# First gathers of a two-block model's expert layers: an earlier start, other buffers and another order of up and value rows

## The chip, the cores and the metric

The kernel runs on one core of one Trainium2 chip. Its time is device time in microseconds (us) for one launch, and three runs of the kernel before took 1977.8, 1981.58 and 1986.32 us. The engines are TensorE (PE in the profile), VectorE (DVE), ScalarE (ACT), GpSimd (POOL) and SyncE (SP); each runs its own instruction list in order and waits on semaphores for the others.

## The reference

Two transformer blocks run one after the other on 256 tokens of width 1024, in float32. The first block has a token mixer (stick-breaking attention and a gated delta rule), a memory cross attention and an expert layer; the second has a gated linear attention, a spatial gating unit and an expert layer. The expert layer is the same in both:

```
q = (xt @ w_pq).reshape(T, 8, 2, 128)                 # 8 heads, two halves
s = einsum('thpd,hpnd->thpn', q, subkeys)             # 128 scores per half
top_s, top_i = top_k(s, 16)                           # per half
best_s, best_pos = top_k(sums of the 16x16 pairs, 16) # 16 experts per head
act = gelu(einsum('thkd,td->thk', peer_u[expert], xb)) * softmax(best_s)
out = einsum('thk,thkd->td', act, peer_v[expert])
```

Each of the 256 tokens reads 128 rows of `peer_u` ("up rows") and 128 rows of `peer_v` ("value rows"), each 1024 floats, from tables of 16384 rows. For a tile of 128 tokens that is 128 gathers of 128 rows per table, so each block makes 512 gathers of 524,288 bytes.

## The kernel before

The tokens are two tiles of 128 (tile 0 and tile 1). Every dense product streams its weight in units of 256 columns (1 MB) into a ring of four slots, `wring`. ScalarE copies a unit to a rounded high part (`K.high`, `w_hi`), VectorE subtracts to get the low part (`K.low`, `w_lo`), and TensorE multiplies high and low parts. The products of the last dense layer before an expert stage are split: its stage does tile 0, and the expert stage does tile 1 on the side (`SecondTile`: four units of eight chunks of three matmuls, L279; `add`, L290, adds a unit's result to the tokens).

The expert stage is `stage_peer`, run twice (`stage 1` from about 391 us, `stage 2` from about 1283 us in the profile). It opens with a fixed sequence. Tile 0 is normalised (`normalise(0)`), transposed (`columns(0)`: TensorE L2220, then a copy of one half on ScalarE, L2072, and one on VectorE, L1948), multiplied with the first query weight (`query(0)`, L2184) and scored against the keys (`score(0)`, L2197). `first_picks` then finds the first eight experts of head 0 on VectorE and writes their numbers into `ex_idx` (L1933). Gathers are indirect DMAs which GpSimd issues: `gather_u(i)` (L2139) brings up row i, `gather_v(j)` (L2151) value row j; i and j count from 0 to 255, sixteen per head and tile (a group). VectorE forms the dot product of each up row (L1994, signal `u_used`), with one part of the eight-part top-16 search of a later head between two rows. When 16 dot products of a group are there, ScalarE applies gelu (L2099), VectorE forms the weights behind the next group's first row (L1959, `weigh`), ScalarE makes a diagonal matrix of each weight (L2114) and TensorE multiplies it with the value row (L2254, signal `v_used_pe` in the order, `pe_used` in the code).

Buffers set the order of the gathers:

- Up rows 0 to 7 go into slots 0 to 7 of `ex_v` and later ones into `wring`, two rows per ring slot. A ring slot comes free when the query weight in it has been used (`home_free(p)`, a wait on `q_ps`, shown as `heads_out_psum`): rows 8 and 9 need query weight 0 gone, rows 14 and 15 weight 3.
- Value rows have 20 slots: 12 in `ex_v`, used first, and 8 in `value_rows`, which hold query weights 4 to 7 until these have been used. Value row 12 takes the slot of value row 0 again, and so on; `gather_v` waits for TensorE to have used the row before it.
- `ex_v` lies where the layer's `XNT`, `w_hi` and `w_lo` were, so GpSimd waits at its start for all four units of the second tile (`second.done`, shown as `projected`).
- The issue order is written in one loop. Six up rows, then for every further i one `gather_v` and one `gather_u(i)`, but no value row at even i in `LEAD_GROWS`.

```
for i in range(U_AHEAD, ROWS):
    if i not in LEAD_GROWS and i < ROWS - TOPK or i % 2:
        gather_v(j)
        j += 1
    gather_u(i)
```

Query weights 4 to 7 are loaded by SP into `value_rows` while the last dense stage runs, 0 to 3 into `wring` (`load_query`, L172). Before the first expert stage, the stages are the cross attention (`stage_cross_attention`, L1326) and its output product.

Of the kernel before, what the change touches and what calls it, by code (L numbers as in the profile page):

```python
# [47 lines left out]
LEAD_GROWS = range(14, 22)  # L48
# [22 lines left out]
class Core:  # L71
# [1254 lines left out]
def stage_cross_attention(K, qT, kT, v_rows, o_pair, fill):  # L1326
# [10 lines left out]
    with ExitStack() as ctx, nc.Block() as block:  # L1337
# [6 lines left out]
        def _(sp):  # L1344
            K.reload(sp, f[-1] + 2)
# [312 lines left out]
def stage_peer(K, rows, sk, nkeys, sk_dma, table_u, table_v, gelu, after, second, queries, out=None):  # L1658
# [23 lines left out]
    with ExitStack() as ctx, nc.Block() as block:  # L1682
# [63 lines left out]
        def value_slot(n):  # L1746
            return more_rows[:, n, :] if n < VRING - RING else rows[:, n - VRING + RING, :]
# [68 lines left out]
        def _(v):  # L1816
# [206 lines left out]
        def _(act):  # L2023
# [52 lines left out]
            K.high(act, PARTS * (second.units[2][0] + 1))  # L2076
# [49 lines left out]
        def _(pool):  # L2126
            def gather_u(i):
# [4 lines left out]
                sig = u_in[i % RING]  # L2132
                if i < RING:
                    sig = v_in[i]
                elif i < 2 * RING:
                    home_free(pool, (i - RING) // 2)
                else:
                    pool.wait_ge(u_used.sem, u_used.at(i - RING + 1))
                nc.gpsimd.indirect_dma_start(u_row(i), None, table_u, bass.IndirectOffsetOnAxis(  # L2139
                    ap=idx[:, g // PH, i % PER_T:i % PER_T + 1], axis=0)).then_inc(sig.sem, 16)  # L2140

            def gather_v(j):
# [6 lines left out]
                elif n < RING:  # L2149
                    pool.wait_ge(u_used.sem, u_used.at(n + 1))  # L2150
# [16 lines left out]
        def _(pe):  # L2167
# [313 lines left out]
```

## Time and profile before

| | |
|---|---|
| median of three runs | 1981.58 us |
| profiled execution | 1986.98 us |
| its span | 1985.3 us |
| TensorE busy | 1625.2 us (82%) |
| VectorE busy | 1263.5 us (64%) |
| ScalarE busy | 607.6 us (31%) |
| GpSimd busy | 1003.0 us (51%) |
| bytes by software (gather) DMA | 536.94 MB |
| bytes by hardware (SP) DMA | 105.88 MB |

The span is what the engines' records cover, the execution's own time 1.7 us more. Matmuls overlap each other, so TensorE's busy share is no measure of how near it is to its peak. The page's row of GB/s cuts the span in 40 slices of 49.6 us.

### The profile page before, as it was taken

How to read it: one execution, taken by the hardware profiler on the slowest of the kernel's cores; microseconds unless marked ns; L12 is line 12 of the kernel's file. 1: busy time of each engine (PE TensorE's matmuls, PEld its weight loads, DVE VectorE, ACT ScalarE, POOL GpSimd, SP SyncE). 2: the span in 40 equal slices, each digit the busy share in tenths (PEclk: the TensorE clock that was granted, in tenths of full speed). 3: DMA queues.
4: the chain of work that ended last, by engine and by line, in shares of the span. 5: the costliest groups of instructions: out<-in, count | busy, mean ns of one | idle time of the engine just before them, and what ended most of it. 6: DMA issues, size and time to landing. Idle time of an engine off the chain costs nothing. (4 is left out here: it accounts for less than half of the span.)

```text
span 1985.3 us, 22064 instructions
## 1 busy us (share of the span) xinstructions
PE 1625.2 (82%) x7643; PEld 1064.7 (54%) x7643; DVE 1263.5 (64%) x2788; ACT 607.6 (31%) x1151; POOL 1003.0 (51%) x1095
## 2 busy tenths in 40 slices
PE   7999999988898667776577899888898667776687
PEld 7998899874453223332233899874453223332233
DVE  6636375588676666676654536687766666666654
ACT  4464544432122122221221446422122122221121
POOL 3012000056777777777764000057777777777764
PEclk9999899998999888888889999998999888888789
DMA  7531355499999999999999563689999999999997
GB/s 240 177 100 45 127 194 191 159 338 368 410 409 409 409 410 409 409 409 410 409 409 365 182 191 107 212 308 388 409 409 409 409 409 409 409 410 410 410 409 282
DMA packets 243719, 644.22 MB, mean 325 GB/s; under 512 B 19541, under 2 KB 105354, under 8 KB 243610
## 3 DMA queue, kind: packets, MB, share of 16 engines
q0 software_dynamic: 147456, 536.94, 68.2%
q1 hardware_dynamic: 96154, 105.88, 16.7%
q8 instruction: 62, 1.02, 0.2%
q14 instruction: 47, 0.39, 0.1%
HBM read 641.69 MB, written 1.05 MB: 324 GB/s over the span
## 5 line engine op out<-in xcount | busy, mean ns | idle before, releaser
L1994 DVE SCALAR_TENSOR_TENSOR ex_uj<-wring,ps 128x1024 f32<-128x1024 f32 x496 | 605.3, 1221 | 406.0 <-DMA wring<-in_peer_u,ex_idx 402.1
L2254 PE MATMUL ps<-ex_v,ex_diag 128*128 128x512 f32 x1336 | 626.7, 627 | 201.6 <-ACT ex_diag L2114 195.5
L2139 POOL DMA_INDIRECT wring<-in_peer_u,ex_idx x496 | 466.9, 941 | 187.6 <-issue 90.9
L2254 PEld LDWEIGHTS ps<-ex_v,ex_diag 128*128 128x128 f32 x1336 | 266.0, 202 | 549.3 <-issue 324.5
L2254 PE MATMUL ps<-value_rows,ex_diag 128*128 128x512 f32 x664 | 310.6, 623 | 101.1 <-ACT ex_diag L2114 96.0
L2151 POOL DMA_INDIRECT ex_v<-in_peer_v,ex_idx x340 | 320.6, 943 | 114.0 <-issue 88.4
L2254 PEld LDWEIGHTS ps<-value_rows,ex_diag 128*128 128x128 f32 x664 | 131.7, 201 | 273.6 <-issue 165.8
L2139 POOL DMA_INDIRECT ex_v<-in_peer_u,ex_idx x16 | 16.4, 1022 | 474.2 <-PE ps L279 469.9
L204 DVE TENSOR_TENSOR w_lo<-wring,w_hi 128x1024 fp32r<-128x1024 f32 (+1 forms) x160 | 187.5, 1212 | 105.0 <-ACT w_hi L195 104.0
L2114 ACT ACTIVATE ex_diag<-ident,ex_weight 128x128 f32<-128x128 f32 x500 | 159.9, 390 | 191.6 <-PE ps L2254 109.0
L2099 ACT ACTIVATE ex_active<-ex_hidden 128x16 f32<-128x16 f32 x32 | 6.9, 215 | 641.9 <-DVE ex_uj L1994 641.9
L2151 POOL DMA_INDIRECT value_rows<-in_peer_v,ex_idx x172 | 161.3, 938 | 52.5 <-issue 46.1
L195 ACT ACTIVATE w_hi<-wring 128x1024 fp32r<-128x1024 f32 (+1 forms) x160 | 158.1, 1039 | 85.7 <-PE ps L562 37.4
L562 PE MATMUL ps<-XNT_high,w_hi 128*128 128x256 f32 x328 | 94.4, 288 | 2.0 <-DVE XNT_low L671 1.4
L562 PE MATMUL ps<-XNT_low,w_hi 128*128 128x256 f32 x328 | 94.0, 287 | 0.0
L562 PE MATMUL ps<-XNT_high,w_lo 128*128 128x256 f32 x328 | 94.0, 287 | 0.0
L241 PE MATMUL ps<-XNT_high,w_hi 128*128 128x256 f32 x288 | 86.4, 300 | 1.0 <-PEq L502 1.0
L241 PE MATMUL ps<-XNT_low,w_hi 128*128 128x256 f32 x288 | 82.7, 287 | 0.0
L241 PE MATMUL ps<-XNT_high,w_lo 128*128 128x256 f32 x288 | 82.6, 287 | 0.0
L562 PEld LDWEIGHTS ps<-XNT_high,w_hi 128*128 128x128 f32 x328 | 63.6, 194 | 2.8 <-DVE XNT_low L671 1.7
L565 PE MATMUL ps<-w_hi,XNT_high 128*128 128x256 f32 (+1 forms) x208 | 59.7, 287 | 5.5 <-DVE XNT_low L627 3.2
L562 PEld LDWEIGHTS ps<-XNT_low,w_hi 128*128 128x128 f32 x328 | 63.6, 194 | 0.0
(455 smaller groups left out, 2449.2 us busy)
## 6 DMA issues: line engine op xcount, KB each, us to landing
wring<-in_w_in SPq DMA_DIRECT2D x42, 1024.0 KB, 5.6
wring<-in_w_ckv SPq DMA_DIRECT2D x8, 1024.0 KB, 5.2
wring<-in_peer_u,ex_idx POOLq DMA_INDIRECT x496, 15.2
ex_v<-in_peer_v,ex_idx POOLq DMA_INDIRECT x340, 13.9
wring<-in_w_mix_out SPq DMA_DIRECT2D x4, 1024.0 KB, 7.2
wring<-in_w_cq SPq DMA_DIRECT2D x4, 1024.0 KB, 5.2
wring<-in_w_co SPq DMA_DIRECT2D x4, 1024.0 KB, 5.3
value_rows<-in_w_pq SPq DMA_DIRECT2D x4, 1024.0 KB, 10.6
```

The source lines that it names most:

```text
L195: self.nc.scalar.activation(self.part(self.w_hi, m, b), self.raw_part(m, b), ACT.Copy).then_inc(self.named("weights_high").sem, 1)
L204: self.nc.vector.tensor_tensor(self.part(self.w_lo, m, b), self.raw_part(m, b), self.part(self.w_hi, m, b).bitcast(F32), ALU.subtract).the ...
L241: last = mm(ps[:, 6 + u % 2, c * S:(c + 1) * S], w[:, i, c * P:(c + 1) * P], x[:, i, :], start=i == 0 and p == 0, stop=i == KD - 1 and p == 2)
L562: last = nc.tensor.matmul(ps[:, j % BANKS, c * S:(c + 1) * S], w[:, i, off + c * P:off + c * P + P], x[:, i, :], start=start, stop=stop, s ...
L565: last = nc.tensor.matmul(ps[:, j % BANKS, c * m:(c + 1) * m], x[:, i, c * P:(c + 1) * P], w[:, i, :], start=start, stop=stop, skip_group_ ...
L1994: ve.scalar_tensor_tensor(out=uj[i % 2], in0=u_row(i), scalar=1.0, in1=tokens(g // PH), op0=ALU.mult, op1=ALU.mult, accum_out=hidden[:, g ...
L2099: nc.scalar.activation(active[:, g % 2, :], hidden[:, g % 2, :], gelu).then_inc(act_r.sem, 1)
L2114: nc.scalar.activation(diag[:, n % DIAGS, :], K.ident[:, :], ACT.Copy, scale=weight[:, g % 2, s:s + 1]).then_inc(dia.sem, 1)
L2139: nc.gpsimd.indirect_dma_start(u_row(i), None, table_u, bass.IndirectOffsetOnAxis(ap=idx[:, g // PH, i % PER_T:i % PER_T + 1], axis=0)).th ...
L2151: nc.gpsimd.indirect_dma_start(value_slot(n), None, table_v, bass.IndirectOffsetOnAxis(ap=idx[:, j // PER_T, j % PER_T:j % PER_T + 1], axi ...
L2254: last = mm(ps[:, 2 * T + c, :], diag[:, n % DIAGS, :], value_slot(v_slot(j))[:, c * BANK:(c + 1) * BANK], start=j % PER_T == 0, stop=ends)
```

## The change

Four things change, in both expert stages unless said otherwise.

1. The opening of the stage. TensorE transposes the keys first, then does unit 0 of the second tile, tile 0's transposes, unit 1, and `query(0)`; before it did units 0 and 1, keys, transposes, two chunks of unit 2 and `query(0)`. ScalarE and VectorE copy the transposed tokens ahead of their work on unit 2.
2. Buffers of the first up rows. Rows 0 and 1 go into the half of `ex_scores` that belongs to tile 1, which need not wait for any unit; rows 2 to 5 go into `ex_v` slots over unit 2's `w_hi` and `w_lo` and wait for unit 2 alone; rows 6 and 7 go into slots 0 and 1. The wait for all units now stands behind the first six gathers. ScalarE's third score copy waits until rows 0 and 1 have been used. The six slots for up rows come last in the list of free value slots, which still has twelve.
3. Order of gathers. Two more value rows go ahead of up row 8 (three at i = 8), and `LEAD_GROWS` ends at 26 instead of 22, so that up rows 22 and 24 have none ahead of them.
4. In the first block only, query weights 4 and 5 are loaded in the cross attention, into a `value_rows` buffer now split in two halves, and weight 7 with 6 in the product after it. The first `merge` writes into `XNT` instead of a pair of its own, which makes the room.

```diff
-LEAD_GROWS = range(14, 22)
+LEAD_GROWS = range(14, 26)
...
+            for n, p in enumerate((4, 5)):
+                K.reload(sp, f[0] + n)
+                K.load_query(sp, queries[0], p, queries[1])
             K.reload(sp, f[-1] + 2)
...
+        w = 2 * (second.units[2][0] % SPLIT)
+        first_slots = [4 + w, 5 + w, 8 + w, 9 + w, 0, 1]
+        free = [n for n in range(VRING - RING) if n not in first_slots] + first_slots
+        u_slots = {i + 2: n for i, n in enumerate(first_slots)}
         def u_row(i):
-            return value_slot(i) if i < RING else ub[:, (first_row + i) % RING, :]
-        free = [(n + RING) % (VRING - RING) for n in range(VRING - RING)]
+            if i < 2:
+                return scores[:, 1, i * D:(i + 1) * D]
+            return value_slot(u_slots[i]) if i in u_slots else ub[:, (first_row + i) % RING, :]
...
             normalise(0)
+            columns(0)
             K.low(v, PARTS * (second.units[2][0] + 1))
             second.add(v)
             second.add(v)
-            columns(0)
...
+                if k == NT:
+                    act.wait_ge(u_used.sem, u_used.at(2))
...
             first_square(0)
-            K.high(act, PARTS * (second.units[2][0] + 1))
             keys(0)
             columns(0)
...
+                if i == 2:
+                    pool.wait_ge(second.done.sem, second.base + 3)
...
-            pool.wait_ge(second.done.sem, second.base + len(second.units))
             for i in range(U_AHEAD):
                 gather_u(i)
+            pool.wait_ge(second.done.sem, second.base + len(second.units))
             j = 0
             for i in range(U_AHEAD, ROWS):
-                if i not in LEAD_GROWS and i < ROWS - TOPK or i % 2:
+                for _n in range(3 if i == RING else 1 if i not in LEAD_GROWS and i < ROWS - TOPK or i % 2 else 0):
                     gather_v(j)
...
-            second.matmuls(pe, 2 * KD)
             keys(0)
+            second.matmuls(pe, KD)
             columns(0)
-            second.matmuls(pe, 2)
+            second.matmuls(pe, KD)
             query(0)
...
-                pm = K.XNT if queries else split_pair("merged", KD, c)
+                pm = K.XNT
...
-                              queries=(A["w_pq"], value_rows, (4, 5, 6)))
+                              queries=(A["w_pq"], value_rows, (6, 7)))
-            stage_peer(..., second, (A["w_pq"], (1, 7, 2, 3)))
+            stage_peer(..., second, (A["w_pq"], (1, 2, 3)))
```

On ScalarE the opening of stage 1 stands like this before (`XN,ex_ss<-X` is the squares of `normalise(0)`, `sk<-ps` the keys, `ex_xT<-ps` its half of the transposed tokens, `w_hi<-wring` one half of a unit):

```order
227 L2057 ACTIVATE XN,ex_ss<-X 128x1024
228 L2060 ACTIVATE ex_sd<-ex_ss,eps 128x1 [waits mean_square_act]
229 L195 ACTIVATE w_hi<-wring 128x1024 [waits projected,weights_in3]
230 L195 ACTIVATE w_hi<-wring 128x1024
231 L2066 ACTIVATE sk<-ps 128x512 [waits keys_psum]
232 L2072 ACTIVATE ex_xT<-ps 128x4x128 [waits transposed_psum]
233 L195 ACTIVATE w_hi<-wring 128x1024 [waits projected,weights_in0]
234 L195 ACTIVATE w_hi<-wring 128x1024
235 L2030 ACTIVATE ex_query<-ps 128x2x128 [waits heads_out_psum]
```

And on ScalarE at the same place now:

```order
227 L2080 ACTIVATE XN,ex_ss<-X 128x1024
228 L2083 ACTIVATE ex_sd<-ex_ss,eps 128x1 [waits mean_square_act]
229 L2089 ACTIVATE sk<-ps 128x512 [waits keys_psum]
230 L2095 ACTIVATE ex_xT<-ps 128x4x128 [waits transposed_psum]
231 L196 ACTIVATE w_hi<-wring 128x1024 [waits projected,weights_in3]
232 L196 ACTIVATE w_hi<-wring 128x1024
233 L196 ACTIVATE w_hi<-wring 128x1024 [waits projected,weights_in0]
234 L196 ACTIVATE w_hi<-wring 128x1024
235 L2051 ACTIVATE ex_query<-ps 128x2x128 [waits heads_out_psum]
```

The two halves of unit 2 have moved from ahead of the keys and the transposed tokens to behind them.

On GpSimd the first gathers of stage 1 stand like this before (`in_peer_u` is an up row, `in_peer_v` a value row, `x5` five in a row; `experts_picked` is the picks, `heads_out_psum` the use of a query weight):

```order
75 L2139 DMA ex_v<-in_peer_u,ex_idx 128x1024 [waits experts_picked,projected]
76 L2139 DMA ex_v<-in_peer_u,ex_idx 128x1024 x5
77 L2151 DMA ex_v<-in_peer_v,ex_idx 128x1024
78 L2139 DMA ex_v<-in_peer_u,ex_idx 128x1024
79 L2151 DMA ex_v<-in_peer_v,ex_idx 128x1024
80 L2139 DMA ex_v<-in_peer_u,ex_idx 128x1024
81 L2151 DMA ex_v<-in_peer_v,ex_idx 128x1024
82 L2139 DMA wring<-in_peer_u,ex_idx 128x1024 [waits heads_out_psum,experts_picked]
```

And on GpSimd now, up to the same up row 8:

```order
75 L2160 DMA ex_scores<-in_peer_u,ex_idx 128x1024 [waits experts_picked]
76 L2160 DMA ex_scores<-in_peer_u,ex_idx 128x1024
77 L2160 DMA ex_v<-in_peer_u,ex_idx 128x1024 [waits projected]
78 L2160 DMA ex_v<-in_peer_u,ex_idx 128x1024 x3
79 L2172 DMA ex_v<-in_peer_v,ex_idx 128x1024 [waits projected]
80 L2160 DMA ex_v<-in_peer_u,ex_idx 128x1024
81 L2172 DMA ex_v<-in_peer_v,ex_idx 128x1024
82 L2160 DMA ex_v<-in_peer_u,ex_idx 128x1024
83 L2172 DMA ex_v<-in_peer_v,ex_idx 128x1024 x3
84 L2160 DMA wring<-in_peer_u,ex_idx 128x1024 [waits u_used,heads_out_psum,experts_picked]
```

Up row 8 was the twelfth gather and is the fourteenth; the wait for the units has moved behind the first gathers.

Further on in GpSimd's list of stage 1, this is the place before where value row 12 (the first with `v_used_pe`) stands:

```order
95 L2139 DMA wring<-in_peer_u,ex_idx 128x1024 [waits u_used,experts_picked]
96 L2151 DMA ex_v<-in_peer_v,ex_idx 128x1024 [waits u_used]
97 L2139 DMA wring<-in_peer_u,ex_idx 128x1024 [waits u_used] x2
98 L2151 DMA ex_v<-in_peer_v,ex_idx 128x1024 [waits u_used]
99 L2139 DMA wring<-in_peer_u,ex_idx 128x1024 [waits u_used] x2
100 L2151 DMA ex_v<-in_peer_v,ex_idx 128x1024 [waits u_used]
101 L2139 DMA wring<-in_peer_u,ex_idx 128x1024 [waits u_used]
102 L2151 DMA ex_v<-in_peer_v,ex_idx 128x1024 [waits v_used_pe]
103 L2139 DMA wring<-in_peer_u,ex_idx 128x1024 [waits u_used]
```

And GpSimd's list now, from the same up row 16 (`experts_picked`) on:

```order
97 L2160 DMA wring<-in_peer_u,ex_idx 128x1024 [waits u_used,experts_picked]
98 L2172 DMA ex_v<-in_peer_v,ex_idx 128x1024 [waits u_used]
99 L2160 DMA wring<-in_peer_u,ex_idx 128x1024 [waits u_used] x2
100 L2172 DMA ex_v<-in_peer_v,ex_idx 128x1024 [waits v_used_pe]
101 L2160 DMA wring<-in_peer_u,ex_idx 128x1024 [waits u_used] x2
102 L2172 DMA ex_v<-in_peer_v,ex_idx 128x1024 [waits v_used_pe]
```

Value row 12 stood behind up rows 0 to 21 and value rows 0 to 11, 34 gathers; it now stands behind up rows 0 to 18 and the same value rows, 31 gathers.

## Rows read from the trace of the kernel before

**Rows 1.** Page, memory traffic of the core in 40 equal slices of the span.
```profile
GB/s 240 177 100 45 127 194 191 159 338 368 410 409 409 409 410 409 409 409 410 409 409 365 182 191 107 212 308 388 409 409 409 409 409 409 409 410 410 410 409 282
```

**Rows 2.** Windows of stage 1: length, busy time per engine, PE clock, DMA share, GB/s.
```profile
409.45:420.00 10.55, 9.09 (x78) 8.49 (x78) 10.31 (x40) 4.19 (x9) 8.41 (x8) 1.00 0.77 254
420.00:455.00 35.00, 21.54 (x127) 19.42 (x126) 30.74 (x97) 8.34 (x19) 24.85 (x27) 0.83 1.03 409
455.00:475.00 20.00, 20.00 (x51) 10.33 (x50) 17.23 (x50) 2.38 (x9) 12.39 (x14) 0.87 0.89 327
...
485.00:495.00 10.00, 7.93 (x19) 3.29 (x18) 5.00 (x11) 1.50 (x6) 7.49 (x8) 1.00 1.00 366
600.00:700.00 100.00, 73.47 (x159) 31.43 (x158) 62.72 (x154) 18.69 (x47) 75.28 (x82) 0.88 1.03 409
```

**Rows 3.** Timeline, POOL, stage 1: start, duration, instruction [idle before <- releaser].
```profile
409.45 1.17 POOL L2139 DMA_INDIRECT ex_v<-in_peer_u,ex_idx  x1 [239.36 <-PE ps L279]
...
424.33 0.94 POOL L2139 DMA_INDIRECT wring<-in_peer_u,ex_idx  x1 [0.30 <-issue]
...
439.19 0.94 POOL L2139 DMA_INDIRECT wring<-in_peer_u,ex_idx  x1 [1.31 <-PE ps L2184]
...
452.85 0.94 POOL L2139 DMA_INDIRECT wring<-in_peer_u,ex_idx  x1 [0.30 <-issue]
458.28 0.94 POOL L2151 DMA_INDIRECT ex_v<-in_peer_v,ex_idx  x1 [4.49 <-PE ps L2254]
...
480.04 0.94 POOL L2151 DMA_INDIRECT ex_v<-in_peer_v,ex_idx  x1 [1.83 <-PE ps L2254]
```

**Rows 4.** Timeline, POOL, stage 2.
```profile
1301.58 0.93 POOL L2139 DMA_INDIRECT ex_v<-in_peer_u,ex_idx  x1 [230.56 <-PE ps L279]
...
1333.09 0.93 POOL L2139 DMA_INDIRECT wring<-in_peer_u,ex_idx  x1 [3.84 <-PE ps L2184]
...
1346.74 0.94 POOL L2139 DMA_INDIRECT wring<-in_peer_u,ex_idx  x1 [0.30 <-issue]
1349.79 0.94 POOL L2151 DMA_INDIRECT ex_v<-in_peer_v,ex_idx  x1 [2.11 <-PE ps L2254]
```

**Rows 5.** Windows of stage 2.
```profile
1330.00:1345.00 15.00, 4.66 (x30) 4.13 (x28) 11.59 (x34) 2.01 (x4) 9.17 (x10) 0.75 0.93 325
...
1350.00:1360.00 10.00, 10.00 (x23) 4.33 (x22) 8.02 (x22) 0.00 (x0) 7.53 (x8) 0.95 0.94 341
```

**Rows 6.** Timeline, DVE, stage 1: norm, picks, up rows 13 and 16, two weights.
```profile
393.05 1.29 DVE L1942 SCALAR_TENSOR_TENSOR XN<-X,ex_iv,gain 128x1024 f32<-128x1024 f32 x1
...
408.35 0.17 DVE L1933 CAST ex_idx<-ex_sel 128x8 int32<-128x8 f32 x1
...
446.06 1.22 DVE L1994 SCALAR_TENSOR_TENSOR ex_uj<-wring,ps 128x1024 f32<-128x1024 f32 x1 [1.32 <-DMA wring<-in_peer_u,ex_idx]
...
452.17 1.21 DVE L1994 SCALAR_TENSOR_TENSOR ex_uj<-wring,ps 128x1024 f32<-128x1024 f32 x1
453.50 0.23 DVE L1959 SCALAR_TENSOR_TENSOR ex_weight<-ex_active,ex_ginv,ex_gate 128x16 f32<-128x16 f32 x1
...
494.02 0.23 DVE L1959 SCALAR_TENSOR_TENSOR ex_weight<-ex_active,ex_ginv,ex_gate 128x16 f32<-128x16 f32 x1
```

**Rows 7.** Timeline, DVE, stage 2: up row 15.
```profile
1341.67 1.22 DVE L1994 SCALAR_TENSOR_TENSOR ex_uj<-wring,ps 128x1024 f32<-128x1024 f32 x1 [1.51 <-DMA wring<-in_peer_u,ex_idx]
```

**Rows 8.** Timeline, PE, stage 1: first unit, keys, transposes, first query, first value rows.
```profile
391.29 0.36 PE L279 MATMUL ps<-w_hi,XNT_high 128*128 128x256 f32 x1 [0.78 <-PEq L502]
...
397.11 0.60 PE L2210 MATMUL ps<-ident,sk 128*128 128x128 f32 x4
397.55 1.04 PE L2220 MATMUL ps<-ident,XN 128*128 128x128 f32 x8
...
399.46 3.81 PE L2184 MATMUL ps<-ex_xT,wring 128*128 128x128 f32 x32
...
454.22 16.92 PE L2254 MATMUL ps<-ex_v,ex_diag 128*128 128x512 f32 x32 [13.46 <-ACT ex_diag L2114]
```

More of the change, by code:

```diff
@@ L165, in query_home @@
         else:
-            flat = rows[:, 2 * (p - RAW):2 * (p - RAW) + 2, :].rearrange("p r d -> p (r d)")
+            n = 2 * ((p - RAW) % 2)
+            flat = rows[(p - RAW) // 2][:, n:n + 2, :].rearrange("p r d -> p (r d)")
         return flat.rearrange("p (k n) -> p k n", k=KD)
@@ L1323, in stage_delta_rule, with stage_cross_attention @@
     K.end_stage()
-def stage_cross_attention(K, qT, kT, v_rows, o_pair, fill):
+def stage_cross_attention(K, qT, kT, v_rows, o_pair, fill, queries):
     nc = K.nc
@@ L1746, in value_slot, with u_signal @@
         def value_slot(n):
-            return more_rows[:, n, :] if n < VRING - RING else rows[:, n - VRING + RING, :]
-        def u_row(i):
-            return value_slot(i) if i < RING else ub[:, (first_row + i) % RING, :]
-        free = [(n + RING) % (VRING - RING) for n in range(VRING - RING)]
+            if n < VRING - RING:
+                return more_rows[:, n, :]
+            half, row = divmod(n - VRING + RING, RING // 2)
+            return rows[half][:, row, :]
+        w = 2 * (second.units[2][0] % SPLIT)
+        first_slots = [4 + w, 5 + w, 8 + w, 9 + w, 0, 1]
+        free = [n for n in range(VRING - RING) if n not in first_slots] + first_slots
+        u_slots = {i + 2: n for i, n in enumerate(first_slots)}
+        def u_row(i):
+            if i < 2:
+                return scores[:, 1, i * D:(i + 1) * D]
+            return value_slot(u_slots[i]) if i in u_slots else ub[:, (first_row + i) % RING, :]
+        def u_signal(i):
+            if i in u_slots:
+                return v_in[u_slots[i]], 1
+            return u_in[i % RING], len([n for n in range(i % RING, i + 1, RING) if n not in u_slots])
         slots = list(free)
@@ L1765, in u_arrived @@
         def u_arrived(v, i):
-            sig, n = (v_in[i], 1) if i < RING else (u_in[i % RING], i // RING)
+            sig, n = u_signal(i)
             v.wait_ge(sig.sem, sig.at(16 * n))
@@ L1790, in v_arrived @@
             n = v_slot(j)
-            eng.wait_ge(v_in[n].sem, v_in[n].at(16 * (v_use(j) + (2 if n < RING else 1))))
+            eng.wait_ge(v_in[n].sem, v_in[n].at(16 * (v_use(j) + (2 if n in first_slots else 1))))
         @block.sync
@@ L2264, in stage_peer @@
             sig.up(by)
-        for sig in u_in:
-            sig.up(16 * (ROWS // RING - 1))
+        for i in range(ROWS):
+            u_signal(i)[0].up(16)
         for j in range(ROWS):
             v_in[v_slot(j)].up(16)
-        for sig in v_in[:RING]:
-            sig.up(16)
     K.gains_used = first_gain + 1 + after
@@ L2376, in program @@
             sk1 = sb("sk1", [P, 2 * PH, P], ctx=first_keys, side="right")
+            value_rows = [sb("value_rows", [P, RING // 2, D], ctx=rows1, side="right")]
             mem = sb("mem", [P, NT, D], ctx=mem_rows, side="right")
@@ L2400, in program @@
                 fill = Filler(K, K.XNT, u_cq, [qT[:, 2 * h:2 * h + 2, :] for h in range(XH)])
-                stage_cross_attention(K, qT, kT, vr, pair, fill)
+                stage_cross_attention(K, qT, kT, vr, pair, fill, (A["w_pq"], value_rows))
                 mem_rows.close()
-                value_rows = sb("value_rows", [P, RING, D], ctx=rows1, side="right")
+                value_rows.append(sb("value_rows", [P, RING // 2, D], ctx=rows1, side="right"))
                 stage_project(K, rows_jobs(K, u_co[0:RAW], pair, K.X, "add", "V", tiles=1), norm_next=True,
-                              queries=(A["w_pq"], value_rows, (4, 5, 6)))
+                              queries=(A["w_pq"], value_rows, (6, 7)))
             second = second_tile(u_co)
             layer.close()
-            stage_peer(K, value_rows, sk1, 2 * PH, sk_dma, A["peer_u"], A["peer_v"], ACT.Gelu, 2, second, (A["w_pq"], (1, 7, 2, 3)))
+            stage_peer(K, value_rows, sk1, 2 * PH, sk_dma, A["peer_u"], A["peer_v"], ACT.Gelu, 2, second, (A["w_pq"], (1, 2, 3)))
             rows1.close()
@@ L2441, in program @@
                     stage_gla_sgu(K, q2, k2, v2, r2, al, su, sv, ya, yb, fill)
-                value_rows = sb("value_rows", [P, RING, D], ctx=rows2, side="right")
+                value_rows = [sb("value_rows", [P, RING // 2, D], ctx=rows2, side="right") for _n in range(2)]
                 merge(u_up2, u_out2, ya, yb, gA, gB, (A["peer_wq"], value_rows, (4, 5, 6, 7)))
```

13 lines of the change are left out of this document (5 added, 8 removed).

## The prediction

> **What bounds the kernel now.** I read the page's traffic row first. It stands at 409 GB/s through most of both expert stages [rows 1], and a window inside one reads 409 GB/s at a DMA share of 1.03 while TensorE, VectorE and GpSimd all have free time [rows 2]. So an expert stage lasts as long as its 512 gathers take to move: 524,288 bytes by 409 GB/s is 1.28 us each, 656 us in all, plus the time in which the memory queues stand empty. An edit at the stage's opening can only change (a) when the bytes start and (b) how long the queues run dry before the steady state.
>
> Next I read the windows near the opening. In stage 1 there are two dips: 327 GB/s over 455 to 475, which loses 20 x 82/409 = 4.0 us, and 366 over 485 to 495, which loses 1.05 us [rows 2]. In stage 2 they are 325 over 1330 to 1345 (3.1 us) and 341 over 1350 to 1360 (1.7 us) [rows 5]. Last I read GpSimd's timeline at these places. In stage 1 it stops once for long: value row 12 goes out at 458.28 after 4.49 us idle, released by TensorE's L2254, while the gather before it left at 452.85 [rows 3]. That is the wait for value row 0 to be used. In stage 2 GpSimd stops at up row 14 (1333.09, 3.84 us, released by the query product L2184) and again at value row 12 (1349.79, 2.11 us) [rows 4].
>
> Are the queues empty when value row 12 goes out? In stage 1, 254 GB/s over 10.55 us and 409 over 35 us have moved 17.0 MB by 455.0 [rows 2]: 32.4 of the 34 gathers issued by then. They run dry near 457, before the row of 458.28. In that case the stage's end is counted from this restart: restart time plus what is left, 512 - 34 = 478 gathers. How early the first gather left no longer matters.
>
> **The change part by part.**
>
> *The opening.* TensorE takes 397.11 - 391.29 = 5.82 us for units 0 and 1, 2.91 each, 0.44 for the keys and 0.79 for the transposes (to 398.34, when the first chunk of unit 2 follows) [rows 8]. In the new order query(0) has keys, unit, transposes and unit ahead of it: 0.44 + 2.91 + 0.79 + 2.91 = 7.05 us, so it starts at 398.4 instead of 399.46. The norm is ready at 394.34 [rows 6], the transposes want it at 394.6: no wait. I take 1.0 us for query, score and picks. GpSimd started 0.93 us behind the end of the picks (408.52 [rows 6], 409.45 [rows 3]); it now waits for these and not for unit 4, so it starts at 408.4. The top-16 search behind the picks gains less, because VectorE's addition of unit 3 stands ahead of it, and TensorE's sum of work up to there is the same but for some 0.3 us of gaps. So rows 0 to 7, which VectorE takes as fast as it can, and the query products come 0.3 us earlier. The new wait of ScalarE for rows 0 and 1 is long met.
>
> *Weights.* Weights 4 and 5 leave in the cross attention, where nothing waits for them; weights 6, 7, 0 and 1 find a shorter queue. The first query starts behind the copied tokens, not behind a weight: nothing. `merge` adds no wait: nothing. If the two megabytes delayed a product's unit, at 409 GB/s they would cost 2 x 2.6 = 5 us at the most.
>
> *Order of gathers.* This is the term that counts. Up to value row 12 there are now 31 gathers, not 34: two more value rows at i = 8, so that the twelve free slots are used up at up row 18 and not 21. The longer `LEAD_GROWS` takes away value rows that stand only behind this point. GpSimd issues one gather per 1.24 us and must wait for weight 3 at up row 14 until about 438.9 (439.19 less 0.3 [rows 3]); seven gathers later, at 447.5, it stands at value row 12 and everything behind it (up row 19 on) waits too. 31 gathers are moved by about 452.
>
> When does value row 12 go now? Its release is row 16's dot product, the weights, the diagonals and TensorE's first value row: 452.17, 453.50, 454.22, 458.28 [rows 3, 6, 8]. VectorE waited for row 13 at 446.06 [rows 6]. That row is now two gathers later (+2.56) in a stream that starts 1.05 earlier: +1.5 us, and the rest of the chain follows, since between rows 13 and 16 VectorE fills the time with its search. Restart: 459.8.
>
> In stage 2 the release hangs on up row 14, which cannot leave before weight 3 is used: 1333.09 less 0.3. Row 15, used at 1341.67 [rows 7], was issued two gathers behind it at 1335.6, so 6.1 us before; the queue is now a little fuller (up to 1 us). Release at -0.3 to +0.7, I take +0.2.
>
> By how much could restart cost more? The first ramp loses 10.55 x 155/409 = 4.0 us [rows 2], and a restart, now as before, happens once: no difference, bounds 0 and, if the dip of before was half hidden by a queue not quite dry, -1.9 us a stage (half of the three gathers).
>
> The Trainium skill (DMA: Bandwidth & Descriptors, Anatomy of one DMA) gives a gather issued from GpSimd 2.0 us plus its bytes by 436 GB/s, 3.2 us here, against the 6.1 us that row 15 took. By the page row 15 would not be waited for in stage 2 and the release would be 0.3 us early, the sum 0.5 us lower; the trace doesn't agree, and I keep its number.
>
> *Second dips.* In stage 1 GpSimd waits 1.83 us at 480.04 for TensorE to use value row 8 [rows 3]. Between rows 12 and 20 there are now 19 gathers instead of 16: it arrives at 459.8 + 19 x 1.24 = 483.4, TensorE is there at 481.5, and the dip of 1.05 us with it is gone; with the short waits at rows 13 and 21, -1.3 us. In stage 2 I take -0.3.
>
> *Sum.* Three gathers more behind the restart, twice 3.85 = 7.7; restart later 1.5 and 0.2; second dips -1.3 and -0.3. Together +7.8 us. Against the profiled execution, 1986.98, that is 1994.8; this execution lies 5.4 us above the median, 1981.58, so for the median 1989.4, 0.39% more. About 0.5% is what the measurement can tell from no change.
>
> **The rivals.**
>
> *Rival 1, the start decides (faster).* If the queues are not really empty at value row 12, each stage gains its earlier start of 1.05, and in stage 2 the two value rows ahead of up row 14 fill the wait of 3.84 us with 2.6 us of bytes: -4.7 us, 1976.9. For it: stage 2 does stop at up row 14, and the first dip there falls just on it. Against it: the restart of stage 1 follows a stop of 4.5 us with a rate of 327 over 20 us, and 1346.74 to 1349.79 shows a second stop in stage 2. It decides if the release comes within about 1 us of GpSimd's arrival, and that it cannot: 447.5 against 459.8.
>
> *Rival 2, the two cancel (no change).* The release moves forward with the opening instead of back, because row 13's wait shrinks in an emptier queue (only 31 gathers compete with it, and all are down by 452): restart -1.0 in both stages, so 7.7 - 2.0 - 1.6 = +4, or less, if a dip is half hidden: 7.7/2 - 2.0 - 1.6 = 0. About 1983.
>
> *Rival 3, the lag carries on (slower).* Up rows 19 to 31 go out three gathers late, so group 1's weights (494.02 [rows 6]) come near 498, and if value row 30, which reuses row 16's slot, then waits too, a second dry spell of 3 us comes in each stage: +13.8, 1995.4. Against it: that row left near 505 (20 gathers behind 480.04 [rows 3]), some 8 us behind its release (494.02 and the first value rows of the group), and both shift alike.
>
> *That the change doesn't do what it says:* the early gathers do leave earlier by the order, so only their worth is in doubt.
>
> **How the numbers follow.** Forecast 0.58 (1985 to 1994), rival 1 0.15, rival 2 0.17, rival 3 0.10. Likeliest 1989.4. The runs of before span 8.5 us, so I add some 2 us on each side: 1978 to 1996 leaves out under half of rival 1 and of rival 3. Slower by over 0.5% means above 1991.5: about a third of the forecast's share and nearly all of rival 3's, 0.30. Faster by over 0.5% means below 1971.7: only the far end of rival 1, 0.05. The rest, 0.65, is within.
>
> **What would show it.** First gather of stage 1 at 408.4, into `ex_scores`; GpSimd idle some 11 us ahead of value row 12 in stage 1 and 8 in stage 2, released by L2254, restart 1 to 2 us later than before in stage 1; a hole in the traffic of about 10 us in place of 5; the short wait near 480 gone. A stage 1 whose traffic has no dip near 450 to 460, or a stage 2 whose only dip is at up row 14, would prove me wrong, as would a release before 457.

## The result, and the profile after

The changed kernel takes 1993.13 us (median of 8 runs, 1989.56 to 1996.43), the kernel before on the same chip 1984.12 (8 runs, 1977.8 to 1987.44): ratio 1.0043, 95% interval 1.0031 to 1.0054. It is 0.4% slower. The profiled execution took 1992.52 us, with a span of 1990.8.

The page's traffic row still stands at 409 GB/s through most of both expert stages. The slice that differs most is the one from 1344 to 1393 us, with the end of stage 2's hole: 336 for 388 [rows 1]. The slice ahead of it has 348 for 308:

```profile
GB/s 243 186 87 45 127 195 230 140 335 341 409 409 409 409 409 409 409 409 409 409 407 361 182 191 106 212 348 336 409 409 409 409 409 409 409 409 410 409 408 279
```

The windows show one wide hole a stage where the kernel before has two narrow ones [rows 2, 5]. Columns: length, busy time of each engine, TensorE's clock, DMA share, GB/s.

```profile
420.00:448.00 28.00, 20.50 (x124) 18.66 (x122) 23.66 (x72) 6.91 (x13) 20.28 (x22) 0.91 1.03 411
448.00:455.00 7.00, 0.99 (x1) 0.50 (x2) 6.96 (x26) 1.66 (x6) 0.00 (x0) 0.50 0.79 314
455.00:470.00 15.00, 15.00 (x31) 6.40 (x30) 8.13 (x22) 2.19 (x8) 9.19 (x10) 0.83 0.66 223
470.00:485.00 15.00, 15.00 (x58) 10.20 (x57) 13.66 (x44) 4.99 (x10) 11.35 (x13) 1.00 1.03 412
...
1315.00:1342.00 27.00, 20.70 (x126) 18.85 (x124) 24.21 (x72) 6.91 (x13) 19.61 (x22) 0.98 1.03 411
1342.00:1350.00 8.00, 2.38 (x3) 1.18 (x4) 7.93 (x30) 3.06 (x11) 0.53 (x1) 0.50 0.57 227
1350.00:1362.00 12.00, 12.00 (x28) 5.28 (x27) 5.82 (x16) 0.79 (x3) 8.04 (x9) 0.96 0.66 224
```

In stage 1 the hole loses 7 x 95/409 + 15 x 186/409 = 8.4 us (1.6 and 6.8) of traffic, where the kernel before lost 4.0 + 1.05 [rows 2]. In stage 2 it loses 3.6 + 5.4 = 9.0 us, where the two dips of before lost 3.1 + 1.7 [rows 5].

GpSimd's timeline of the changed kernel, at the places of [rows 3, 4] (first gather, up rows 13 and 14, the last gather ahead of value row 12, value row 12; then the first gather, up row 14 and value row 12 of stage 2):

```profile
407.82 1.17 POOL L2160 DMA_INDIRECT ex_scores<-in_peer_u,ex_idx  x1 [237.52 <-DVE ex_idx L1954]
...
437.03 0.94 POOL L2160 DMA_INDIRECT wring<-in_peer_u,ex_idx  x1 [0.30 <-issue]
438.93 0.94 POOL L2160 DMA_INDIRECT wring<-in_peer_u,ex_idx  x1 [0.96 <-PE ps L2205]
...
446.39 0.94 POOL L2160 DMA_INDIRECT wring<-in_peer_u,ex_idx  x1 [0.30 <-issue]
458.07 0.94 POOL L2172 DMA_INDIRECT ex_v<-in_peer_v,ex_idx  x1 [10.73 <-PE ps L2275]
...
1303.02 0.94 POOL L2160 DMA_INDIRECT ex_scores<-in_peer_u,ex_idx  x1 [228.82 <-DVE ex_idx L1954]
...
1334.12 0.94 POOL L2160 DMA_INDIRECT wring<-in_peer_u,ex_idx  x1 [1.29 <-PE ps L2205]
...
1351.52 0.94 POOL L2172 DMA_INDIRECT ex_v<-in_peer_v,ex_idx  x1 [8.98 <-PE ps L2275]
```

GpSimd comes to value row 12 early and then stands 10.73 and 8.98 us, for 4.49 and 2.11 before. VectorE's timeline has the chain that releases it, as in [rows 6]: up row 13, up row 16, the weight; and the stage's last addition, which ends stage 1.

```profile
445.85 1.22 DVE L2015 SCALAR_TENSOR_TENSOR ex_uj<-wring,ps 128x1024 f32<-128x1024 f32 x1 [1.33 <-DMA wring<-in_peer_u,ex_idx]
...
451.94 1.22 DVE L2015 SCALAR_TENSOR_TENSOR ex_uj<-wring,ps 128x1024 f32<-128x1024 f32 x1
453.29 0.23 DVE L1980 SCALAR_TENSOR_TENSOR ex_weight<-ex_active,ex_ginv,ex_gate 128x16 f32<-128x16 f32 x1
...
1094.07 1.22 DVE L1986 TENSOR_TENSOR X<-X,ps 128x1024 f32<-128x1024 f32 x1
```

The restart is 0.2 us earlier than before in stage 1 (458.07 for 458.28), not 1.5 later. These are times from the start of the span, and the stage itself does not open at the same time in two executions. So below, the restart is counted from the second query product on TensorE, query(1), which stands at these places before and after:

```profile
408.60 3.73 PE L2184 MATMUL ps<-ex_xT,wring 128*128 128x128 f32 x32
408.33 3.73 PE L2205 MATMUL ps<-ex_xT,wring 128*128 128x128 f32 x32
```

From the restart to the last addition are 1094.07 - 458.07 = 636.00 us; before, its last addition stood at 1091.12, so 632.84:

```profile
1091.12 1.22 DVE L1965 TENSOR_TENSOR X<-X,ps 128x1024 f32<-128x1024 f32 x1
```

### The profile page after: what moved, and what is told of

It is laid out like the page before. It is cut to its first block and busy times, and to the rows that moved or that the text cites. A ratio compares the mean times of both kernels' runs of the same rounds, so it can differ in the third digit from the quotient of the medians.

```text
span 1990.8 us, 22066 instructions
## 1 busy us (share of the span) xinstructions
PE 1627.7 (82%) x7643; PEld 1063.7 (53%) x7643; DVE 1263.2 (63%) x2788; ACT 608.8 (31%) x1151; POOL 1006.3 (51%) x1095
## 3 DMA queue, kind: packets, MB, share of 16 engines
HBM read 641.69 MB, written 1.05 MB: 323 GB/s over the span
## 5 line engine op out<-in xcount | busy, mean ns | idle before, releaser
L2275 PE MATMUL ps<-ex_v,ex_diag 128*128 128x512 f32 x1336 | 633.6, 632 | 202.4 <-ACT ex_diag L2136 195.8
L2160 POOL DMA_INDIRECT ex_scores<-in_peer_u,ex_idx x4 | 4.0, 997 | 466.9 <-DVE ex_idx L1954 466.3
L566 PE MATMUL ps<-w_hi,XNT_high 128*128 128x256 f32 (+1 forms) x272 | 78.7, 289 | 6.9 <-DVE XNT_low L628 4.6
L566 PE MATMUL ps<-w_hi,XNT_low 128*128 128x256 f32 (+1 forms) x272 | 78.0, 287 | 0.0
L566 PE MATMUL ps<-w_lo,XNT_high 128*128 128x256 f32 (+1 forms) x272 | 78.0, 287 | 0.0
```

The lines of the kernel that those rows point to most:

```text
L566: last = nc.tensor.matmul(ps[:, j % BANKS, c * m:(c + 1) * m], x[:, i, c * P:(c + 1) * P], w[:, i, :], start=start, stop=stop, skip_group_ ...
L2275: last = mm(ps[:, 2 * T + c, :], diag[:, n % DIAGS, :], value_slot(v_slot(j))[:, c * BANK:(c + 1) * BANK], start=j % PER_T == 0, stop=ends)
```

## The experiments

Three settings tell the kernels apart: the *opening* (all of the change but the order of gathers), *three at 8* (three value rows ahead of up row 8), and how many gathers stand *ahead* of value row 12. Before is old opening, no three, 34. After is new opening, three, 31. "Idle" is GpSimd's idle time just ahead of value row 12, stages 1 and 2.

| run | opening | three at 8 | ahead | ratio to before | 95% interval | idle, us |
|---|---|---|---|---|---|---|
| before | old | no | 34 | 1 | | 4.49, 2.11 |
| after | new | yes | 31 | 1.0043 | 1.0031 to 1.0054 | 10.73, 8.98 |
| e12 (after again) | new | yes | 31 | 1.0046 | 1.0031 to 1.0060 | 11.68, 9.09 |
| e7 order only | old | yes | 31 | 1.0056 | 1.0037 to 1.0075 | 10.51, 8.87 |
| e6 opening only | new | no | 34 | 0.9975 | 0.9963 to 0.9988 | 2.27, 1.10 |
| e11 late start | new | no | 34 | 0.9995 | 0.9983 to 1.0007 | 2.42, 1.98 |
| e10 | new | yes | 34 | 1.0012 | 1.0001 to 1.0023 | 7.58, 5.41 |
| e9 | new | yes | 37 | 0.9976 | 0.9965 to 0.9987 | 3.68, 1.48 |
| e8 | new | no | 37 | 0.9974 | 0.9964 to 0.9984 | 0.30, 0.30 |
| e5 | old | no | 37 | 0.9995 | 0.9982 to 1.0009 | 0.30, 0.30 |

Each ratio is to the kernel before as it ran beside that experiment: 1983.53 us (29 runs) beside e5 to e8, which ran on one chip, and 1984.46 (29 runs) beside e9 to e12, which ran on another. The first four experiments fell on a third chip, on which the kernel before took 2149.61 us (15 runs), 8% more; they are told last.

**e6_opening_again: the new opening with the old order.**

```diff
-LEAD_GROWS = range(14, 26)
+LEAD_GROWS = range(14, 22)
-                for _n in range(3 if i == RING else 1 if i not in LEAD_GROWS and i < ROWS - TOPK or i % 2 else 0):
+                for _n in range(1 if i not in LEAD_GROWS and i < ROWS - TOPK or i % 2 else 0):
```

> The kernel after with the order of gathers of the kernel before (34 ahead), once more. Dry queue, with the releases as the trace after showed them (restart 0.2 us earlier in the first stage, 1.5 us earlier against its stage's opening in the second): 1.7 us faster than before, ratio 0.998 to 1.001. Start decides: 3 us faster, 0.998 to 0.999. If the opening costs something of its own whatever the chip (as the first run of it, 1.0048 where gathers moved at about 365 GB/s, would have it): 1.003 to 1.006, and GpSimd waits some 10 us ahead of up row 8 here too.

Measured: 1978.02 us against 1983.53, ratio 0.9975. This beats both kernels, and it lies just outside all three expectations: the opening is worth 5 us (interval 2 to 7), more than the 1.7 of the dry-queue theory and the 3 of "start decides". There is no wait of 10 us ahead of up row 8 (0.30 at 418.30).

**e7_order_again: the old opening with the new order.**

```diff
-LEAD_GROWS = range(14, 22)
+LEAD_GROWS = range(14, 26)
-                if i not in LEAD_GROWS and i < ROWS - TOPK or i % 2:
+                for _n in range(3 if i == RING else 1 if i not in LEAD_GROWS and i < ROWS - TOPK or i % 2 else 0):
```

> The kernel before with the order of gathers of the kernel after (31 ahead), once more. Dry queue: 2 x 3.85 us slower, ratio 1.003 to 1.005. If the order cost nothing and the opening is what made the kernel after slower: 0.999 to 1.001.

Measured: 1.0056, some 11 us slower (interval 7 to 15), by the median a little above the range of the dry-queue theory. The loss of the changed kernel comes from the order, all of it, and the opening pays back about half: 1.0056 and 0.9975 add up to 1.0031, the changed kernel itself has 1.0043.

**e12_after_again: the changed kernel beside others, unchanged.**

> The kernel after once more, unchanged, beside the others. The order alone was 1.0056 and the opening alone 0.9975 of the kernel before; if the two add up: 1.003, 1.002 to 1.0045. If they don't (the opening gains nothing where the queue runs dry behind it): 1.0045 to 1.0065.

Measured: 1.0046 (1.0031 to 1.0060), at the edge between the two expectations. So this run can't tell a plain sum (1.0031) from a sum in which a little of the opening is lost; it confirms the size of the loss.

**e10_34_three_at_8: three at 8, but 34 ahead.** The edit against the changed kernel:

```diff
-LEAD_GROWS = range(14, 26)
+SKIPS = (14, 16, 18, 19, 20, 21)
-                for _n in range(3 if i == RING else 1 if i not in LEAD_GROWS and i < ROWS - TOPK or i % 2 else 0):
+                for _n in range(3 if i == RING else 1 if i not in SKIPS and (i < ROWS - TOPK or i % 2) else 0):
```

> The kernel after with its three value rows ahead of up row 8 kept, and 34 gathers ahead of value row 12 (no value row between up rows 18 to 21). Dry queue: the run with the opening alone (0.9975) less the dip at up row 14 (4.5 us at 343 GB/s in the second stage, 0.8 us in the first), plus up to 1.5 us a stage since up row 16 lands behind two more value rows: ratio 0.995 to 0.998. If what counts is only the start of the gathers: 0.9975, 0.997 to 0.999.

Measured: 1.0012, a miss. I expected the bytes that fill the dip at up row 14 to be a gain; with the count of gathers equal to e6, the kernel is 0.37% slower (7 us, between medians of two chips). GpSimd's and VectorE's timelines show a part of it. First e6: up rows 13 and 14 and value row 12 leave; then VectorE uses up rows 13 and 16.

```profile
430.72 1.13 POOL L2160 DMA_INDIRECT wring<-in_peer_u,ex_idx  x1 [0.30 <-issue]
435.30 0.94 POOL L2160 DMA_INDIRECT wring<-in_peer_u,ex_idx  x1 [3.45 <-PE ps L2205]
...
452.18 0.94 POOL L2172 DMA_INDIRECT ex_v<-in_peer_v,ex_idx  x1 [2.27 <-PE ps L2275]
```

```profile
439.96 1.22 DVE L2015 SCALAR_TENSOR_TENSOR ex_uj<-wring,ps 128x1024 f32<-128x1024 f32 x1 [1.28 <-DMA wring<-in_peer_u,ex_idx]
...
446.06 1.22 DVE L2015 SCALAR_TENSOR_TENSOR ex_uj<-wring,ps 128x1024 f32<-128x1024 f32 x1
```

The same of e10:

```profile
433.44 0.94 POOL L2160 DMA_INDIRECT wring<-in_peer_u,ex_idx  x1 [0.31 <-issue]
435.34 0.94 POOL L2160 DMA_INDIRECT wring<-in_peer_u,ex_idx  x1 [0.97 <-PE ps L2205]
...
455.03 0.94 POOL L2172 DMA_INDIRECT ex_v<-in_peer_v,ex_idx  x1 [7.58 <-PE ps L2275]
```

```profile
443.21 1.22 DVE L2015 SCALAR_TENSOR_TENSOR ex_uj<-wring,ps 128x1024 f32<-128x1024 f32 x1 [1.33 <-DMA wring<-in_peer_u,ex_idx]
...
449.31 1.21 DVE L2015 SCALAR_TENSOR_TENSOR ex_uj<-wring,ps 128x1024 f32<-128x1024 f32 x1
```

These two executions run level up to here: query(1) starts on TensorE at 404.71 and 404.75, and up row 14, which waits for TensorE, leaves at 435.30 and 435.34. But with three at 8 row 13 leaves 2.72 us later and is used 3.25 later; rows 14 to 16 follow at VectorE's pace, and value row 12 goes 2.85 us later. The two value rows are not free filling: they stand ahead of the up rows whose dot products release value row 12. From query(1) to the stage's end e10 is longer than e6 by 2.6 us in stage 1 and 0.6 in stage 2; that is 3.2 of the 7 us, and the rest isn't explained.

Against e12, which ran beside it and differs only in the three gathers (31 ahead), e10 is 0.34% faster, 6.7 us. This is the plainest test of the prediction's main term, 2 x 3.85, and it bears it out.

**e9_37_three_at_8: three at 8 and 37 ahead.** As e10, with more up rows taken ahead:

```diff
-LEAD_GROWS = range(14, 26)
+SKIPS = (14, 16, 18, 19, 20, 21, 22, 23, 24)
```

> The kernel after with its three value rows ahead of up row 8 kept, and up rows 19, 21 and 23 without a value row between them, so that 37 gathers stand ahead of value row 12 in place of 31. Dry queue: no dip at value row 12, as with 37 ahead before (0.9974 and 0.9995), and the dip at up row 14 filled as well (1315 to 1342 us at 411 in place of 366 GB/s = 2.9 us in the second stage, 0.5 us in the first): some 8 us faster than the kernel before, ratio 0.994 to 0.9975. If the dip at up row 14 is given back behind it: as the run with 37 ahead, 0.997 to 0.999.

Measured: 0.9976, just outside the first expectation and within the second. Against e10, the three gathers more that go out ahead of the same late release are worth 0.36%, 7 us: what the dry-queue theory gives them (2 x 3.85).

**e8_37_again: new opening, no three, 37 ahead** (against the changed kernel: `SKIPS = (14, 16, 18, 20, 22, 23, 24)`, and no three at 8).

> The kernel after with 37 ahead of value row 12, once more. Dry queue: against the kernel after six gathers fewer behind each restart, 2 x 6 x 1.28 = 15.4 us less, so 6.5 us faster than before, ratio 0.995 to 0.998, where gathers move at 409 GB/s. Opening costs of its own: 1.000 to 1.003.

Measured: 0.9974, as the dry-queue theory had it against before, but the same as e6 with 34. Where the release comes early (idle 2.27 and 1.10), three more gathers ahead buy nothing that the timed runs can tell from no change; by the traces the two stages are 1.9 us shorter.

**e5_before_37_ahead: the old kernel with 37 ahead.**

```diff
-LEAD_GROWS = range(14, 22)
+SKIPS = (14, 16, 18, 20, 22, 23, 24)
-                if i not in LEAD_GROWS and i < ROWS - TOPK or i % 2:
+                if i not in SKIPS and (i < ROWS - TOPK or i % 2):
```

> The kernel before with 37 gathers ahead of value row 12 in place of 34: up rows 22 to 24 go ahead of it, the opening and the homes of the rows are untouched. Dry queue: three gathers fewer are left at each restart, 3 x 1.28 = 3.85 us a stage, but a stage can't gain more than its dip loses at row 12: 20 us at 327 in place of 409 GB/s = 4.0 us in the first, 10 us at 341 = 1.7 us in the second. So 5.5 to 7.7 us faster, ratio 0.996 to 0.997, where gathers move at 409 GB/s; on a chip where they move slower the queue dries less and the gain is smaller, 0.998 to 1.000. Start decides: no change, 0.999 to 1.001.

Measured: 0.9995, a miss of the first expectation. GpSimd doesn't stop at value row 12 any more, and the dip there is gone, and from query(1) to the last addition stage 1 is 2.7 us shorter by the trace, stage 2 1.3. Of this the timed runs show 1 us, with an interval from 3.6 us faster to 1.8 slower. A part of the 2.7 us isn't the edit's: GpSimd's list is the same as before up to value row 12, and yet up row 13, issued at the same distance from query(1) (407.19 here, so +28.35 in both), is used 1.43 us earlier, and the weights follow it:

```profile
435.54 0.94 POOL L2139 DMA_INDIRECT wring<-in_peer_u,ex_idx  x1 [0.30 <-issue]
```

```profile
443.22 1.22 DVE L1994 SCALAR_TENSOR_TENSOR ex_uj<-wring,ps 128x1024 f32<-128x1024 f32 x1 [1.33 <-DMA wring<-in_peer_u,ex_idx]
...
450.66 0.23 DVE L1959 SCALAR_TENSOR_TENSOR ex_weight<-ex_active,ex_ginv,ex_gate 128x16 f32<-128x16 f32 x1
```

At the end of stage 1 the last gather lies 22.7 us before the last addition in place of 21.0, so part of the dip's worth may be given back there; no run tests it.

**e11_late_start: as e6, but the first gather waits for all units, as before the change.**

```diff
+            pool.wait_ge(second.done.sem, second.base + len(second.units))
             for i in range(U_AHEAD):
                 gather_u(i)
-            pool.wait_ge(second.done.sem, second.base + len(second.units))
```

> The opening alone (order of the kernel before, 34 ahead), but GpSimd waits for all units of the projection before its first gather, as the kernel before does. If an earlier start carries through to the end (as the traces of the runs have it, against the prediction): 1.1 to 1.5 us a stage later than with the opening alone, 0.9985 to 1.0005. If it doesn't count (as predicted): the same as the opening alone, 0.9965 to 0.9985.

Measured: 0.9995 for 0.9975 with the early start; the intervals just overlap. The times speak for a start that counts; the trace does not: value row 12 of stage 1 goes out 47.62 us behind query(1), for 47.47 in e6, though the first gather left 0.97 us later (at +0.46 for -0.51); in stage 2 it goes at +47.14, earlier than e6's +47.90. That profiled execution was the fastest of its twelve (1975.99, median 1982.39), so it may not be typical. Open.

**The first four, on the chip where the kernel before takes 2149.61 us.** They are the edits of e6 (e1), e7 (e2) and e8 (e4), and the changed kernel with 29 ahead (e3, `SKIPS = (16, 18, 20, 22, 24, 26)`).

> The changed kernel with the gather order of before: one value row ahead of up row 8, LEAD_GROWS to 22, so value row 12 has 34 gathers ahead of it again; the opening, the buffers and the query loads stay as changed. Dry-queue theory (a stage's end is counted from the release of value row 12, and what matters is how many gathers stand ahead of it and when it is released): the 7.7 us come back, and the release is up to 1.7 us earlier per stage than before, so -1 to -4 us against the kernel before, 1980 to 1983. Rival (the opening and the buffers themselves cost the time, the order does nothing): about +8.5, like the changed kernel. Rival (the start decides): -2 to -5, and the order-only kernel below is then no slower than before.

> The kernel before with nothing changed but the order of gathers: three value rows ahead of up row 8 and LEAD_GROWS to 26, so value row 12 has 31 gathers ahead of it. Dry-queue theory: three gathers twice, +7.7 us, and a release 1 to 2 us later in stage 1 because up rows 8 to 16 come two gathers later without the earlier start; second dips shorter by 1.3: +7 to +10 us against before, at least as slow as the changed kernel. Rival (opening and buffers cost): 0. In stage 2 the stop at up row 14 should shrink to about 1.3 us by either theory.

> The changed kernel with value row 12 moved further forward: one more value row between up rows 13 and 14, so 29 gathers stand ahead of it instead of 31; the lead of the up rows is the same again from up row 27 on. Dry-queue theory: two gathers twice is +5.1 us, and rows 14 to 16 one gather later up to +1.2 a stage: +5 to +7.5 against the changed kernel, +13.5 to +16 against before; GpSimd idle 13 us ahead of value row 12 in stage 1. Rival (only the opening counts, or DMA work is what it is): same as the changed kernel.

> The changed kernel with value row 12 moved back: no value row ahead of up rows 14, 16, 18, 20, 22, 23 and 24, so that it stands behind up rows 0 to 24 and value rows 0 to 11, 37 gathers, and the up rows keep a lead of three more for the rest of the stage. Dry-queue theory: three gathers more than in the opening-only kernel, twice 3.85 us, so -7.7 against it and -9 to -12 against before, 1972 to 1975, as long as the queue still runs dry ahead of the release; if it no longer does, the gain stops short of that (-5 to -8). Rival (only the start decides): same as the opening-only kernel.

Measured: e1 1.0048 (1.0028 to 1.0067), e2 1.0084 (1.0066 to 1.0102), e3 1.0131 (1.0109 to 1.0153), e4 1.0057 (1.0038 to 1.0077). That is 10, 18, 28 and 12 us slower than before, and none of the four is what the dry-queue theory expected of it. By the medians the order costs more here, and 29 ahead most; 37 ahead buys nothing over e1, as in e8; but the opening costs, where it gains on the other chips. Timelines of e1: TensorE between query(1) and the keys' transposes, ScalarE's copy of query(1), GpSimd at up row 8.

```profile
407.11 3.73 PE L2205 MATMUL ps<-ex_xT,wring 128*128 128x128 f32 x32
410.68 1.04 PE L2231 MATMUL ps<-ident,sk 128*128 128x128 f32 x8
419.44 1.12 PE L2231 MATMUL ps<-ident,sk 128*128 128x128 f32 x4 [7.73 <-issue]
```

```profile
415.25 0.39 ACT L2051 ACTIVATE ex_query<-ps 128x256 f32<-128x256 f32 x1 [6.00 <-remote]
```

```profile
433.12 0.94 POOL L2160 DMA_INDIRECT wring<-in_peer_u,ex_idx  x1 [12.92 <-DVE ex_uj L2015]
```

ScalarE's copy of query(1) starts 4.4 us behind TensorE's last product for it (415.25 for 410.84), a wait for which the profile names no engine of the core; TensorE, VectorE and at last GpSimd stand behind it. In e6, the same program on another chip, neither wait is there. The new opening is not needed for them: in e2, with the old one, ScalarE's copy of query(2) stands at 422.62 behind such a wait of 12.09 us. What they are, and whether they make the opening's loss here, wasn't settled: no run here takes them away.

## Why the prediction was right

Forecast 1989.4 in a range of 1978 to 1996, measured 1993.13; forecast +7.8 us, measured +9.0 by the medians. The main term was right. Of the smaller ones the restart of stage 1 can't be told from its forecast, the restart of stage 2 and the second dips were off, in opposite ways. So that the sum lies within 1.2 us of the result is in part luck.

The timed runs cut the change into three steps, e6, e10, e12: the opening -5 us, two value rows ahead of up row 8 +7, three gathers fewer ahead of value row 12 +7 (each give or take some 3 us). The prediction had -1.05 and +2.56 for the first two in stage 1, +0.2 for both together in stage 2, and +7.7 for the third. The first two are both larger in the runs, and largely cancel.

*Three gathers more behind the restart, 3.85 us a stage: right.* Every trace outside the slow session agrees. From value row 12 to the last addition of stage 1, the kernels with 34 ahead take 632.84 (before), 632.12 (e6), 631.87 (e10) and 632.05 us (e11); with 31 ahead, 636.00 (after), 636.09 (e7) and 636.81 (e12). The means differ by 4.1. From value row 12 of stage 2 to the end they are 635.1 and 639.1: 4.0. The openings and the dips ahead of it make under 1 us of difference to this stretch, so the queue is dry at the restart and the end is counted from it. The rows are GpSimd's and VectorE's; of e7 and e12:

```profile
459.24 0.94 POOL L2151 DMA_INDIRECT ex_v<-in_peer_v,ex_idx  x1 [10.51 <-PE ps L2254]
...
1356.45 0.94 POOL L2151 DMA_INDIRECT ex_v<-in_peer_v,ex_idx  x1 [8.87 <-PE ps L2254]
```

```profile
1095.33 1.22 DVE L1965 TENSOR_TENSOR X<-X,ps 128x1024 f32<-128x1024 f32 x1
```

```profile
456.09 0.94 POOL L2172 DMA_INDIRECT ex_v<-in_peer_v,ex_idx  x1 [11.68 <-PE ps L2275]
...
1352.16 0.94 POOL L2172 DMA_INDIRECT ex_v<-in_peer_v,ex_idx  x1 [9.09 <-PE ps L2275]
```

```profile
1092.90 1.22 DVE L1986 TENSOR_TENSOR X<-X,ps 128x1024 f32<-128x1024 f32 x1
```

*Second dips, -1.3 and -0.3: wrong.* The dip near 480 did go (412 GB/s over 470 to 485), but the stretches behind the restart, which hold it, grew by 4.1 and 4.0 and not by 2.6 and 3.6: 1.05 us of the second dip in stage 1 did not come back in the whole; where they went isn't shown.

*Restart 1.5 later in stage 1: not refuted.* Value row 12, counted from query(1), leaves at +49.68 before, +49.74 and +50.66 in the two traces of the changed kernel: +0.5 us on average. But the trace of before is one of two of the same program up to here. The weights that release value row 12 are formed at +44.90 before and at +43.47 in e5; with the new opening and three at 8 they come at +44.96 (after), +45.88 (e12), +45.89 (e10) and +45.97 (e9). The averages differ by 1.5 us, as forecast. One trace a side can't settle a difference of this size, since row 13 lands up to 1.4 us apart in the same program. In absolute time e12's restart, 456.09, is even earlier than the 457 that was to prove me wrong, with query(1) at 405.43: that sign should have been counted from query(1).

Of its two halves, three at 8 is the surer. With the new opening the weights come at +42.69 and +42.55 in e6 and e8, some 3 us before those of the four traces with three at 8: the two value rows' own time, 2.56, and a little more. The opening, with the old order, brings them 0.8 to 2.4 us earlier. That this is the early start isn't shown: in e11 the first gather waits as it did before, and the weights still come at +42.84.

*Restart 0.2 later in stage 2: wrong, and for a reason that is not in the sum.* It leaves at +48.91 before and at +47.97 and +48.03 after, 0.9 us earlier. The prediction hangs it on up row 14, and took that row's place, behind query weight 3, as given. It leaves 32.21 us behind query(1) before and 30.57 after, because query(2) on TensorE takes 9.01 us before and 7.38 after:

```profile
1309.09 9.01 PE L2184 MATMUL ps<-ex_xT,wring 128*128 128x128 f32 x64 [2.37 <-DVE ex_xT L1948]
1311.76 7.38 PE L2205 MATMUL ps<-ex_xT,wring 128*128 128x128 f32 x64 [2.38 <-DVE ex_xT L1969]
```

```profile
1309.00:1318.00 9.00, 8.91 (x65) 8.94 (x66) 8.90 (x29) 3.38 (x6) 6.70 (x8) 0.81 1.00 384
1311.76:1320.76 9.00, 9.00 (x75) 8.85 (x76) 8.90 (x31) 4.24 (x8) 6.79 (x8) 1.00 1.02 403
```

The granted clock is 0.81 over these 9 us before, and 1.00 after, with TensorE idle for some 2.4 us ahead of them in both. Before, it stands at the lower of its two levels, 1.2 GHz, from 1311 to 1313, of which this is the first half:

```profile
1311.00:1312.00 1.00, 1.00 (x7) 1.00 (x7) 0.93 (x4) 0.00 (x0) 0.69 (x2) 0.50 1.01 360
```

Of the ten traces (before, after, e5 to e12) the slow query(2) of stage 2 is in all three with the old opening (before, e5, e7) and in one of seven with the new (e6; not in e8, the same program up to there). Whether the opening decides it can't be said from so few.

*The opening: start 408.4, measured 407.82*, and 1.36 us nearer to query(1) than before. In stage 1 up row 14 leaves 30.6 us behind query(1) in each of the ten traces in which GpSimd waits there (all but e7's, where GpSimd comes to it at 32.1), so the earlier start doesn't pass that wait. Whether it passes by an emptier queue is what e11 leaves open.

*Rival 1, the start decides,* was wrong for this change, since the release came 11 us behind GpSimd's arrival. Its -4.7 us is near the -5 that e6 measured for the opening, but 2.6 of them were the bytes of the two value rows, which e6 doesn't have and which e10 shows to be a loss. *Rival 2* had a restart 1.0 earlier in both stages, from a row that lands sooner in an emptier queue. Stage 2's is 0.9 earlier, but up row 13 is used later there than before (+35.91 for +34.82, behind query(1)); what is earlier is up row 14. *Rival 3* did not come: TensorE waits 5.13 us for group 1's diagonals at 497.68 for 2.07 before, but GpSimd stands nowhere for more than 0.3 us between 459 and 558.

*The landing of a row.* By the Trainium skill (DMA: Bandwidth & Descriptors, Anatomy of one DMA), 2.0 us plus the bytes by 436 GB/s, such a gather would take 3.2 us, an estimate. Here too loaded queues take longer: up row 13, for which VectorE waits, is used 8.8 us behind its issue in the changed kernel (437.03, 445.85) and 9.2 in e6 (430.72, 439.96), and 6.5 to 9.8 us over both stages of the ten traces.

*Where trace and medians part.* From query(1) to the end of each stage, summed, the changed kernel is 6.1 and 7.3 us longer than before in its two traces, e6 4.7 shorter, e7 8.8 longer, e8 6.6 shorter; the timed runs say 8.5 and 9.1, 5.0, 11, 5.2. All these but e6's come out lower than the timed runs, so the single trace of before is likely some 2 us long; e5's trace, 1.4 us shorter up to the weights of stage 1 with the same program, points the same way.

## What to carry to other kernels

Where a stage is bound by traffic, find the wait at which the queue runs dry and count two things: how many transfers are left behind it, and what sets its release. Moving transfers ahead of that wait gains their full time as long as the issuing engine stands idle there for longer than it takes to issue them (7 us for three a stage, 3.7 us of issuing, at 7.6 and 5.4 us idle; 1 us, within the noise, at 4.5 and 2.1; nothing to be measured at 2.3 and 1.1), unless they stand in front of the very transfers that release it. Time a change in parts: here one half gained 5 us and the other lost 11, and the half alone, with the old order, is the faster kernel (1978.02 us for 1983.53).

## What was not expected of the hardware

The same program took 1984 us in three sessions and 2150 in a fourth, on another chip; there a window of the steady state moves 366 GB/s (e1, 600 to 700) for 409, and an engine stands for 6 to 13 us at places where it doesn't elsewhere. Whether this is the chip or something else that ran on it, no run shows.

Stretches in which the program is the same vary by more than the effects sought: query(1) of stage 1 starts between 403.19 and 408.65 in the ten traces outside that session, and stage 1's last addition to query(1) of stage 2 takes 209.1 to 211.9 us, with no relation to the edit that I can see. A difference of 4 us is to be read stretch by stretch, from a point that both traces share, and one of 1 us not from a single pair of traces.
